# A hybrid encoder layer on one core: a second weight buffer in the first attention block, and attention outputs turned one unit later in another PSUM bank

## The chip, the cores and the metric

The kernel runs on one core of a Trainium2 chip. A core has five engines with queues of their own: TensorE (matrix products; PE in the profile, its weight loads PEld), VectorE (DVE), ScalarE (ACT), GpSimd (POOL) and SyncE (SP, which only issues transfers). They meet at semaphores, and 16 DMA engines move data between HBM and the on-chip memory SBUF. TensorE writes to PSUM, which has eight banks of 512 fp32 columns in each of 128 partitions. The metric is the device time of one execution in microseconds, lower is better.

## What is computed

One step of a layer with 1024 prompt rows and 32 sample rows of 1024 values, all in fp32:

```python
xn = rmsnorm(x, norm1_g);  z = xn @ w_in              # conv B | conv C | conv h | q | k | v | gates
a  = (B * dwconv3_causal(C * h)) @ w_conv_out
q, k = rope(rmsnorm(q)), rope(rmsnorm(k))             # 8 heads, two components of 64 each
o_h = (softmax(Q1 K1^T) - lam * softmax(Q2 K2^T)) V   # chunk-causal; values of 128
b  = (rmsnorm(o, subln_g) * (1 - lam0)) @ w_attn_out
x  = x + (sigmoid(gA) * a + sigmoid(gB) * b) @ w_o
x  = x + PEER(rmsnorm(x, norm2_g))                    # 8 heads choose 16 of 16384 experts each per row
```

PEER takes, for every row and each of its 128 chosen experts, a dot product with one row of a table, a GELU and a gate, and adds as much of a second row. Keys, values and the last two convolution inputs are outputs too.

## The kernel before

**Blocks and stages.** The 1056 rows are nine tiles of 128 (the last has the 32 sample rows), in three blocks of three tiles. Every block goes through an *attention* part and a *middle* part (gates, output projections, second norm, PEER queries and their top 16). The expert work is cut into 1056 *slots*: in slot q POOL gathers for each of 128 rows one 8 KB row pair of the expert table into entry q % 8 of a ring (half of the ring in `mix`, half in `ringx`), VectorE takes the dot product (L1588), ScalarE makes GELU, gate and a diagonal of 64 columns (L1212 to L1223), and TensorE adds the weighed second half to the accumulator in banks 0 and 1 (L1001), or, for a part of the slots, VectorE does (L1599). A ring entry is free for the next gather after that.

**What sets the order.** Each engine's program is one loop over slots from -340 to 1055. The parts of the three blocks are generators that yield a slot number ahead of each step; a step is issued in the loop once its number has passed (`advance`). Steps of one generator keep the order of the code whatever their numbers are. The attention of a block has a table of its own, `ATT` with start and pace: the first block runs in slots -330 to -141, ahead of all gathers, the second in 25.5 to 167, the third in 337 to 513. A *unit* u = 3h + i is head h with tile i of the block; it takes 7 positions, and a position is 1.0, 0.75 or 0.93 of a slot in the three blocks. The constants of lines 48 to 59 give the position of every step in its unit.

**A unit of attention.** TensorE's order in unit u is: scores of u (`score`, L776, both components, into banks 2 to 5), values weighed for u-1 (`weigh_values`, L831, bank 7), queries and keys of u+1 turned (`turn_heads`, L845 and L846, columns 0 to 255 of bank 6), projection of q, k and v for unit u+3 (`project`, L797, columns 0 to 383 of bank 6), in the first block one of three convolution products per tile (`conv_block`, L858), the normalised output of u-1 turned (`turn_out`, L838, bank 4, position `TO`), and the softmax weights of u turned (`turn_weights`, L812, bank 7). ScalarE copies turned heads (`keep_heads`, L1091 and L1092), squares the output (L1065, `square_out`), takes the exponential (L1047), copies and squares new projections (L1081, L1084), copies the turned output (`keep_out`, L1071) and the turned weights (L1060). VectorE takes row maxima (L1395), scales heads (L1446), multiplies the output by its gain (`keep_product`, L1456), forms the difference of the softmaxes (L1404 to L1410), applies the norm (`norm_out`, L1462), and rotates (L1429 to L1435). POOL makes the reciprocal roots (L696 to L707).

Because the turned output goes to bank 4, which the second component's scores use, the turning waits for the exponential of unit u, and the scores of the next unit wait for the copy (`ot_c`). The projection waits for the copies of the turned heads (`tq_c`), since they share bank 6.

**Weights.** `low` holds six blocks of 1024 columns. In the first block its first three hold the q, k and v weights of one head, and the last three those of a convolution channel group; SyncE loads them in the order of `attend(0)`:

```python
                    for h in range(-1, DC):
                        if 0 <= h < DC - 1:
                            for k in range(3):
                                load_conv(h + 1, k)
                        if 0 <= h + 2 < DC:
                            if h >= -1:
                                load_heads(h + 2)
```

`load_conv` waits for the convolution product that used the buffer, `load_heads(g)` for all three projections of head g-1. In the second and third block there are no convolution loads in this part, and even and odd heads have three columns blocks of `low` each.

## Time and profile before

| | us |
|---|---|
| median of 3 runs | 4035.53 |
| the runs | 4030.66, 4035.53, 11249.31 |
| profiled execution | 4040.45 |
| its span (first to last instruction) | 4038.5 |

| engine | busy us | share of the span |
|---|---|---|
| TensorE matmul | 3205.6 | 79% |
| VectorE | 2685.7 | 67% |
| GpSimd | 1550.3 | 38% |
| ScalarE | 1460.6 | 36% |

The core moved 1345 MB; 1107 MB of them are gathers. The mean granted clock of TensorE was 0.866 of full speed. In a row of the timeline the columns are start, duration, engine, line, operation, output and inputs, the number of instructions merged, and in brackets the idle time before it with what ended it. A row of waits says: engine, tile and line that waited, on whom, us in total, number of times, the longest. Busy times are those of one profiled execution.

### The profile page before, as it was taken

How to read it: one execution, taken by the hardware profiler on the slowest of the kernel's cores; microseconds unless marked ns; L12 is line 12 of the kernel's file. 1: busy time of each engine (PE TensorE's matmuls, PEld its weight loads, DVE VectorE, ACT ScalarE, POOL GpSimd, SP SyncE). 2: the span in 40 equal slices, each digit the busy share in tenths (PEclk: the TensorE clock that was granted, in tenths of full speed). 3: DMA queues.
4: the chain of work that ended last, by engine and by line, in shares of the span. 5: the costliest groups of instructions: out<-in, count | busy, mean ns of one | idle time of the engine just before them, and what ended most of it. 6: DMA issues, size and time to landing. Idle time of an engine off the chain costs nothing.

```text
span 4038.5 us, 46682 instructions
## 1 busy us (share of the span) xinstructions
PE 3205.6 (79%) x14264; PEld 1449.4 (36%) x14264; DVE 2685.7 (67%) x6248; ACT 1460.6 (36%) x4353; POOL 1550.3 (38%) x1402
## 2 busy tenths in 40 slices
PE   6888997877886999898788887876779766666666
PEld 3444554433343555344233332544425211111111
DVE  3333103888888976578778886886668864566664
ACT  2111101245665234232456555223433333333332
POOL 1111000344665433333445555443354443444433
...
GB/s 194 78 75 80 126 99 135 294 350 331 356 385 368 410 417 418 380 396 307 313 351 354 387 347 347 416 411 365 406 413 410 366 420 419 420 420 420 410 393 341
DMA packets 258104, 1345.41 MB, mean 333 GB/s; under 512 B 31489, under 2 KB 71169, under 8 KB 122433
## 3 DMA queue, kind: packets, MB, share of 16 engines
...
q1 hardware_dynamic: 80720, 210.05, 14.1%
...
## 4 chain that ended last, share of the span: by engine, by line
PE 40%; DMA 24%; DVE 20%; ACT 5%; issue 4%; DVEq 3%; POOL 2%; SPq 1%; ACTq 1%; POOLq 0%
DMA ringx<-in_peer_uv,tl_idx 12%; DMA mix<-in_peer_uv,tl_idx 10%; PE tl_ps L951 9%; PE tl_ps L1001 7%; PE tl_ps L797 6%; DVE ringx L1588 3%; PE tl_ps L962 3%; PE tl_ps L935 3%; PE tl_ps L986 3%; PE tl_ps L858 3%; DVE mix L1588 3%; DVE tl_xa L1599 2%; PE tl_ps L776 2%; DMA low<-in_watt 1%; DVE tl_mx L1395 1%
## 5 line engine op out<-in xcount | busy, mean ns | idle before, releaser
L734 POOL DMA_INDIRECT mix<-in_peer_uv,tl_idx x528 | 630.7, 1194 | 768.8 <-PE tl_ps L1001 426.2
L734 POOL DMA_INDIRECT ringx<-in_peer_uv,tl_idx x528 | 621.7, 1177 | 722.3 <-PE tl_ps L1001 454.6
L1588 DVE CUSTOM_DVE_ANT_0 mix<-mix,tl_xb 128x1024 f32<-128x1024 f32 x528 | 641.5, 1222 | 281.6 <-DMA mix<-in_peer_uv,tl_idx 273.6
L1588 DVE CUSTOM_DVE_ANT_0 ringx<-ringx,tl_xb 128x1024 f32<-128x1024 f32 x528 | 641.0, 1221 | 271.6 <-DMA ringx<-in_peer_uv,tl_idx 264.0
L1001 PE MATMUL tl_ps<-ringx,tl_dg 64*64 64x512 f32 x3352 | 577.2, 773 | 279.6 <-ACT tl_dg L1223 279.0
L1212 ACT ACTIVATE tl_hg<-tl_hd 128x1 f32<-128x1 f32 x1056 | 213.1, 202 | 1558.4 <-DVE tl_hd L1588 1548.3
L1001 PE MATMUL tl_ps<-mix,tl_dg 64*64 64x512 f32 x3288 | 565.5, 772 | 259.5 <-ACT tl_dg L1223 239.1
L951 PE MATMUL tl_ps<-tl_xr,low 128*128 128x384 f32 (+1 forms) x1280 | 401.0, 469 | 27.2 <-DMA low<-in_wall 22.8
L1216 ACT ACTIVATE tl_hw<-tl_hg,tl_gw 128x1 f32<-128x1 f32 x1056 | 310.9, 294 | 76.2 <-issue 4.7
L1001 PEld LDWEIGHTS tl_ps<-ringx,tl_dg 64*64 64x64 f32 x3352 | 106.3, 156 | 614.8 <-ACT tl_dg L1223 533.4
L797 PE MATMUL tl_ps<-low,tl_xr 128*128 128x384 f32 (+1 forms) x768 | 298.5, 536 | 25.3 <-ACT tl_u L1092 20.1
L951 PEld LDWEIGHTS tl_ps<-tl_xr,low 128*128 128x128 f32 x1280 | 246.6, 196 | 195.8 <-issue 67.7
L1001 PEld LDWEIGHTS tl_ps<-mix,tl_dg 64*64 64x64 f32 x3288 | 105.0, 157 | 588.0 <-ACT tl_dg L1223 482.8
L1223 ACT ACTIVATE tl_dg<-tl_eye,tl_hw 128x64 f32<-128x64 f32 x830 | 288.7, 348 | 59.5 <-issue 2.6
L986 PE MATMUL tl_ps<-tl_xr,low 128*128 128x384 f32 (+1 forms) x768 | 262.1, 480 | 1.9 <-ACTq L1184 1.9
L935 PE MATMUL tl_ps<-tl_xr,low 128*128 128x384 f32 (+1 forms) x768 | 237.1, 467 | 0.6 <-ACT tl_xr L1071 0.6
L797 PEld LDWEIGHTS tl_ps<-low,tl_xr 128*128 128x128 f32 (+1 forms) x768 | 137.0, 189 | 192.8 <-issue 99.7
L705 POOL TENSOR_SCALAR tl_rr<-tl_ss 128x4 f32<-128x4 f32 (+1 forms) x72 | 61.5, 854 | 370.9 <-DVE tl_ss L1416 370.8
L797 PE MATMUL tl_ps<-low,mix 128*128 128x384 f32 x384 | 151.7, 555 | 55.7 <-DMA low<-in_watt 41.6
L986 PEld LDWEIGHTS tl_ps<-tl_xr,low 128*128 128x128 f32 x768 | 139.6, 194 | 135.3 <-issue 75.0
L935 PEld LDWEIGHTS tl_ps<-tl_xr,low 128*128 128x128 f32 x768 | 149.8, 199 | 101.9 <-issue 34.7
L1553 DVE TENSOR_TENSOR tl_u<-tl_ps,tl_u 128x384 f32<-128x384 f32 (+1 forms) x48 | 25.0, 521 | 197.7 <-PE tl_ps L951 195.6
...
## 6 DMA issues: line engine op xcount, KB each, us to landing
...
```

What stands on the lines that cost most here:

```text
L734: nc.gpsimd.indirect_dma_start(out=ring[q % RING].rearrange("p a d -> p (a d)"), out_offset=None, in_=A["peer_uv"], in_offset=bass.Indirec ...
L797: last = nc.tensor.matmul(o, xn[:, c, i * P:i * P + n], w[:, :, c, :], start=(c == 0), stop=(c == DC - 1))
L858: last = nc.tensor.matmul(ps[:, (3, 5, 3)[k], 0:nr], w[:, c, :], xn[:, c, 0:nr], start=(c == 0), stop=(c == DC - 1))
L935: last = nc.tensor.matmul(ps[:, 2 + 3 * (cc % 2) + k, 0:n], w[:, c, :], xnr[:, c, 0:n], start=(c == 0), stop=(c == DC - 1))
L951: last = nc.tensor.matmul(ps[:, 2 + k, 0:n], w[:, c, :], src[k][:, c, 0:n], start=(c == 0), stop=(c == DC - 1))
L962: last = nc.tensor.matmul(ps[:m, 2 + 2 * i + h, :], mixT[:, c, i * P:i * P + m], low_block(keep, (base + 32 + c) % WRING)[:, h * 512:(h + ...
L986: last = nc.tensor.matmul(ps[:, 2 + qb % 2, 0:n], w[:, c, :], xT[:, c, 0:n], start=(c == 0), stop=(c == DC - 1))
L1001: last = nc.tensor.matmul(ps[half_of(h), b, :], dg[rows, npe(q) % DIAGS, :], ring[q % RING][rows, 1, h * 512:(h + 1) * 512], start=k == 0, ...
L1212: nc.scalar.activation(hg[:, j:j + 1], hd[:, j:j + 1], ACT.Gelu)
L1216: gate = nc.scalar.activation(hw[:, j:j + 1], hg[:, j:j + 1], ACT.Copy, scale=gw[:, table(t), k:k + 1])
L1223: nc.scalar.activation(dg[:, npe(q) % DIAGS, :], eye[:], ACT.Copy, scale=hw[:, j:j + 1]).then_inc(s["dg_done"], 1)
L1588: nc.vector.tensor_tensor_reduce(out=ring[q % RING][:, 0, :], in0=ring[q % RING][:, 0, :], in1=xb[:, t % 2, :], scale=1.0, scalar=0.0, op0 ...
```

## The change

Three things are done.

1. In the first block odd heads' weights get a buffer of their own, columns 2304 to 5375 of `ringx` (`heads_at`), behind the rotary tables that lie there. `load_heads(1)` waits for nothing, `load_heads(g)` for the projections of heads up to g-2, and SyncE issues it ahead of the convolution loads of a head. Counts of the semaphores follow.
2. In all blocks the output of unit u-2 is turned in unit u, between the weighing of values and the turning of heads, into columns 384 to 511 of bank 6. ScalarE copies it ahead of the turned heads, once these are in PSUM too. The scores don't wait for that copy any more, the projection does. The last output of a block is turned at its old position.
3. Positions: the turning of heads and the copies of the turned heads move from 1.8 and 2.3 to 0.8 and 1.3, the product of output and gain from 2.2 to 3.2. The scaling of heads stays at 1.0.

```diff
-PV, TO, PJ, TQ, CV = 1.0, 5.0, 2.6, 1.8, 3.6
+PV, TO, PJ, TQ, CV = 1.0, 5.0, 2.6, 0.8, 3.6
-RO, KP = 2.2, 1.2
+RO, KP, SH = 2.2, 2.2, 1.0
...
+        def heads_at(rb, par):
+
+            if rb == 0 and par:
+                return ringx[:, (NT + 1) * 4 * HD:(NT + 1) * 4 * HD + 3 * D]
+            return keep["low"][:, 3 * par * D:3 * (par + 1) * D]
...
             def load_heads(g):
 
-                rb, par = g // DC, g % 2 if g >= DC else 0
-                if rb == 0:
-                    sp.wait_ge(s["pj_done"], 3 * g)
-                elif g % DC == 0:
+                rb, par = g // DC, g % 2
+                if g and g % DC == 0:
                     sp.wait_ge(s["z_done"], BASE[rb])
-                else:
+                elif g > 1:
                     sp.wait_ge(s["pj_done"], 3 * (g - 1))
...
                 if rb == 0:
-                    for h in range(-1, DC):
...
+                    load_heads(1)
+                    for h in range(DC - 1):
+                        if h + 2 < DC:
+                            load_heads(h + 2)
+                        for k in range(3):
+                            load_conv(h + 1, k)
                     return
...
                def score(g, i, components):
-                        if w >= 2:
-                            pe.wait_ge(s["ot_c"], w - 1)
...
                def project(g, i):
                             if j > DC * 3 * rb:
                                 pe.wait_ge(s["tq_c"], max(j - 1, 3 * DC * rb))
+                                if j > 4:
+                                    pe.wait_ge(s["ot_c"], j - 4)
...
-                def turn_out(g, i, seen):
-                    n = rows_of(tiles[i])
+                def turn_out(g, i):
+                    n, latest = rows_of(tiles[i]), min(3 * g + i + 5, 3 * DC * (rb + 1))
                     pe.wait_ge(s["on_d"], 3 * g + i + 1)
-                    pe.wait_ge(s["ex_d"], seen)
-                    nc.tensor.transpose(ps[:, 4, 0:n], on[:n, :], ident[:n, :n]).then_inc(s["to_d"], 1)
+                    for name in ("qn_d", "v_cp", "sq_d"):
+                        pe.wait_ge(s[name], latest)
+                    pe.wait_ge(s["tq_c"], min(3 * g + i + 3, 3 * DC * (rb + 1)))
+                    if 3 * g + i:
+                        pe.wait_ge(s["ot_c"], 3 * g + i)
+                    nc.tensor.transpose(ps[:, 6, 3 * P:3 * P + n], on[:n, :], ident[:n, :n]).then_inc(s["to_d"], 1)
...
+                    if u > 1:
+                        yield step_at(rb, h, base + TQ)
+                        turn_out(DC * rb + (u - 2) // 3, (u - 2) % 3)
                     if -2 < u < 3 * DC - 1:
                         yield step_at(rb, h, base + TQ)
                         turn_heads(DC * rb + (u + 1) // 3, (u + 1) % 3)
...
-                    if u > 0:
+                    if u == 3 * DC:
                         yield step_at(rb, h, base + TO)
...
                 def keep_out(g, i):
                     n = rows_of(tiles[i])
                     act.wait_ge(s["to_d"], 3 * g + i + 1)
-                    nc.scalar.copy(oT[:, g % DC, i * P:i * P + n], ps[:, 4, 0:n]).then_inc(s["ot_c"], 1)
+                    act.wait_ge(s["tq_d"], min(3 * g + i + 4, 3 * DC * (rb + 1)))
+                    nc.scalar.copy(oT[:, g % DC, i * P:i * P + n], ps[:, 6, 3 * P:3 * P + n]).then_inc(s["ot_c"], 1)
...
+                    if u > 1:
+                        yield step_at(rb, h, base + TQ + 0.5)
+                        keep_out(DC * rb + (u - 2) // 3, (u - 2) % 3)
                     if 0 <= after[0] < DC:
                         yield step_at(rb, h, base + TQ + 0.5)
                         keep_heads(DC * rb + after[0], after[1])
```

## Rows read from the trace of the kernel before

**Rows 1.** Stretches: engines' busy us, clock, DMA share, GB/s.
```profile
core 0: us, PE busy (x) PEld busy (x) DVE busy (x) ACT busy (x) POOL busy (x), PEclk, DMA share, GB/s
60.00:425.00 365.00, 308.36 (x1046) 180.69 (x1046) 140.90 (x501) 69.03 (x291) 51.93 (x94) 0.93 0.24 82
812.00:1293.00 481.00, 382.57 (x2024) 175.70 (x2024) 416.59 (x993) 268.09 (x758) 263.65 (x235) 0.90 0.92 356
1880.00:2508.00 628.00, 500.45 (x2545) 201.82 (x2545) 495.01 (x1044) 333.87 (x892) 321.65 (x273) 0.86 0.91 352
3200.00:3900.00 700.00, 439.07 (x2224) 81.78 (x2220) 434.14 (x821) 248.56 (x845) 296.30 (x276) 0.71 1.01 418
```
**Rows 2.** Waits of TensorE, 60 to 425 us: total, times, longest.
```profile
PE tl_ps L797 <- DMA low<-in_watt: 41.6, 7, 6.8
```
**Rows 3.** Timeline of TensorE: projections of one head, and the next.
```profile
264.37 7.97 PE L797 MATMUL tl_ps<-low,mix 128*128 128x384 f32 x16 [6.19 <-DMA low<-in_watt]
...
279.87 5.43 PE L797 MATMUL tl_ps<-low,mix 128*128 128x384 f32 x16 [0.52 <-ACT tl_u L1092]
...
293.27 5.43 PE L797 MATMUL tl_ps<-low,mix 128*128 128x384 f32 x16 [0.52 <-ACT tl_u L1092]
```
**Rows 4.** Timeline of SyncE's queue in that head: the load waited for.
```profile
256.42 1.38 SPq L529 DMA_DIRECT2D low<-in_watt  x3
```
**Rows 5.** Timeline of SyncE's queue at the start of the first block.
```profile
58.01 0.62 SPq L608 DMA_DIRECT2D tl_xr<-xn_t  x1
67.44 1.29 SPq L529 DMA_DIRECT2D low<-in_watt  x3
```
**Rows 6.** Timeline of TensorE: the first projection that waits for weights.
```profile
73.61 6.81 PE L797 MATMUL tl_ps<-low,mix 128*128 128x384 f32 x13 [4.32 <-DMA low<-in_watt]
```
**Rows 7.** Timeline, first block: scores behind idle time (TensorE), copies (ScalarE).
```profile
242.76 0.27 ACT L1071 COPY tl_xr<-tl_ps 128x128 f32<-128x128 f32 x1 [4.72 <-PE tl_ps L838]
...
243.13 0.92 PE L776 MATMUL tl_ps<-tl_u 64*128 64x384 f32 x4 [0.18 <-issue]
...
244.94 0.27 ACT L1091 COPY tl_u<-tl_ps 128x128 f32<-128x128 f32 x1 [1.59 <-PE tl_ps L846]
245.10 0.27 ACT L1092 COPY tl_u<-tl_ps 128x128 f32<-128x128 f32 x1
...
278.01 0.70 PE L776 MATMUL tl_ps<-tl_u 64*128 64x256 f32 x4 [0.29 <-issue]
```
**Rows 8.** Waits of TensorE in the second block, 812 to 1293 us.
```profile
PE tl_ps L838 <- DVE tl_u L1462: 21.6, 9, 5.1
PE tl_ps L797 <- ACT tl_u L1092: 14.1, 10, 4.0
```
**Rows 9.** Waits of VectorE in the second block.
```profile
DVE tl_u L1429 <- ACT tl_u L1084: 11.5, 7, 2.8
DVE tl_u L1456 <- ACT tl_u L1065: 5.7, 2, 3.1
DVE tl_rz L1404 <- ACT tl_u L1047: 5.1, 7, 1.5
```
**Rows 10.** Waits of TensorE in the third block, 1880 to 2508 us.
```profile
PE tl_ps L838 <- DVE tl_u L1462: 16.6, 9, 3.6
PE tl_ps L797 <- ACT tl_u L1092: 6.0, 4, 2.8
```
**Rows 11.** Waits of VectorE in the third block.
```profile
DVE tl_mx L1395 <- PE tl_ps L776: 27.5, 12, 4.7
DVE tl_u L1429 <- ACT tl_u L1084: 23.9, 13, 6.2
DVE tl_u L1456 <- ACT tl_u L1065: 16.0, 10, 4.7
DVE tl_rz L1404 <- ACT tl_u L1047: 13.0, 9, 2.2
DVE ringx L1588 <- DMA ringx<-in_peer_uv,tl_idx: 6.6, 4, 2.5
```
**Rows 12.** A wait of ScalarE in the second block.
```profile
ACT tl_u L1091 <- PE tl_ps L846: 12.8, 13, 2.5
```

21 lines of the change are left out of this document (7 added, 14 removed).

## The prediction

> **What bounds the kernel now.** I read the stage table first (busy time per engine, granted clock, DMA share by stretch), because what a saved microsecond is worth depends on the stage. It shows three regimes [rows 1]. From 60 to 425 us the first block's attention runs alone: TensorE is busy 308 of 365 us, DMA is nearly idle at 0.24, and no expert rows are gathered yet, so the stretch is a chain on TensorE. From 812 to 1293 us and from 1880 to 2508 us the attention of the second and the third block runs between the gathers: DMA share 0.92 and 0.91 at 356 and 352 GB/s, VectorE 417 of 481 and 495 of 628 us. From 3200 to 3900 us the DMA is full (1.01, 418 GB/s); nothing on an engine is worth anything there. The bounds of the mixed stretches are the slots of the step tables (25.5 to 167 and 337 to 513), counted off by VectorE's dot products. So the change, which touches attention only, can pay in the first stretch fully and in the two mixed ones as far as DMA and VectorE allow. Everything behind runs by slot number and not by the clock, so a saved microsecond moves all that follows; the next weights' loads move with it.
>
> The waits of TensorE in the first stretch come next: 41.6 us in seven waits for head weights [rows 2]. The timeline shows what one costs [rows 3]: the projection at 264.37 starts after 6.19 us of idle, and its 16 matmuls then take 7.97 us, where the unstalled ones (279.87, 293.27) take 5.43 and wait only 0.52 us for a ScalarE copy. Start to start, unstalled units are 13.40 us apart (279.87 to 293.27). Why the weights are late: SyncE works its queue in order, its last convolution load waits until the block's third convolution product is done, and the three head loads stand behind it, issued at 256.42, when they need about 8 us to land [rows 4]. With one buffer they could not go before the projection that reads it had ended in any case.
>
> Last I read who makes TensorE and VectorE wait in the mixed stretches. TensorE waits 21.6 and 16.6 us at the turning of the outputs (L838) for their normalisation on VectorE, and 14.1 and 6.0 us before a projection for the copies of the turned heads [rows 8, 10]. VectorE hardly waits for gathers there (6.6 us of 628 for the ring's second half in the third block); its waits are those inside attention [rows 9, 11].
>
> **Part 1: second buffer in the first block.** Odd heads' weights go to columns 2304 to 5375 of the ring, which gathers fill only after the first block. The first odd load waits for nothing now; its neighbours in SyncE's queue are the table stores and one reload issued at 58 us, and today it is issued at 67.44 and waited for from 69.29 (73.61 - 4.32) [rows 5, 6]. A load takes about 8 us from issue to use [rows 4], so it arrives in time or within 1 us of it. Later loads wait for the projections of two heads before, and come ahead of the convolution loads in the queue, so they have one whole head period (some 40 us) to land. The convolution loads now stand behind a wait for projections that end before the convolution product they wait for, and they are wanted 35 us later: cost nothing, covered by the period. The same bytes move, at a DMA share of 0.24. Removed: 41.6 us of waits less 7 x 0.52 us, the copy wait that then ends last, is 38.0 us. The slow matmuls too: in the row at 264.37 they cost 7.97 - 5.43 = 2.54 us. The granted clock of the stretch is 0.93 [rows 1]: TensorE falls from its level of 2.4 GHz to that of 1.2 GHz in the six microseconds without matmuls, and the first part of the next projection is run there; behind the waits of 0.52 us no projection is slow. With the stalls gone I take all of it: 7 x 2.54 = 17.8 us. Part 1: 55.8 us. Bounds: 38.0 (the clock falls anyway) to 56.
>
> **Part 2: outputs turned one unit later, in bank 6.** *In the first block.* The scores start 0.18 to 0.29 us after the weight transposes, because today the copy of the turned output out of bank 4 must be done [rows 7]; that wait goes, 23 times 0.23 us, 5.4 us. The transposition itself only moves, from ahead of the scores to behind them, on the same chain. Added is one more ScalarE copy ahead of the two that the next projection waits for anyway; such copies start 0.16 us apart (244.94, 245.10) [rows 7]: 23 x 0.16 = 3.7 us. Net gain 1.7 us; bounds -4 (nothing of the first is seen) to +5. The wait for the normalised output is away by construction: it is a unit (13 us) old.
>
> The rule that speaks against this part is that of the Trainium skill, page "PSUM — Partial Sum Buffer", section "PSUM bank collisions raise a hardware error": two engines may not be in one bank and quadrant at once, even on different columns, so the free columns of bank 6 are not a free bank. Read strictly, no copy may overlap another engine's work in the bank and each is paid whole: by the rows 0.27 in place of 0.16 us, 6.2 in place of 3.7 us, and part 2 would lose 1 us here in place of winning 1.7. The copies in the rows overlap with each other, being of one engine, so I stay with 0.16.
>
> *In the second and third block.* TensorE loses its waits of 21.6 + 16.6 us at L838, and the 14.1 + 6.0 us before projections shrink, since the turning of heads moves from position 1.8 to 0.8 of the 7 positions of a unit (a position is 0.75 and 0.93 of a slot there) while the projection stays at 2.6. But TensorE is not what ends last; it is busy 383 of 481 us and then waits for ScalarE's slot weights. So I count what VectorE, the busiest at 0.87, stops waiting for. L1456 (output times gain) moves from 2.2 to 3.2, and ScalarE's square that it waits for moves from 2.3 (behind the copies of the heads) to 1.6: all of 5.7 and 16.0 us go [rows 9, 11]. L1404 waits for the exponential, which stood behind the same copies and the square, about 0.5 us of copies: I take 4 of 5.1 and 8 of 13.0. L1429 waits for the projection: with 36 us of TensorE's waits gone in the second block I take 8 of 11.5, in the third, where only 23 go, 12 of 23.9. Row maxima waiting for scores in the third block: most of the 27.5 I put down to the sample tile's second component, which waits for the first one's exponential; 7. Sum 18 + 43 = 61 us. Half of it I give back: a VectorE that comes earlier meets the next wait earlier, and DMA has only 8 to 9% to give. That leaves 30 us. Bounds: none of it (0) to 61 us, and as a ceiling the DMA rate of the full stretches, 481 x (1 - 356/418) + 628 x (1 - 352/418) = 71 + 99 us.
>
> Queues: SyncE's loads in these blocks stay in place. ScalarE gets the output copy ahead of the head copies, one of 0.27 us and in the place of one that it had later; behind it stand square, exponential and the slot's gate. POOL's order is unchanged; its reciprocal root of the output now finds the square done earlier.
>
> **Sum.** 55.8 + 1.7 + 30 = 87.5 us. The profiled execution took 4040.45 us (span 4038.5), 4.9 us over the median of 4035.53; 4040.5 - 87.5 = 3953 on its scale, 3948 on that of the median.
>
> **Rivals.** (All on the median's scale.)
> *A, only part 1 pays: 4035.5 - 57.5 = 3978 us, chance 0.31.* For it: DMA share 0.92 is close to full, and TensorE is not the bound in the mixed stretches, so its waits may only change names. Against: VectorE, not the gathers, is waited for there. [...]
> *B, the mixed stretches give all of it: 4035.5 - 57.5 - 61 = 3917 us, chance 0.17.* For it: the ceiling of 170 us leaves room, and the clock of these stretches (0.90, 0.86) may rise with fewer gaps. Against: four waits in a row rarely all go.
> *C, slower: 4098 us, chance 0.05.* One mechanism: ScalarE. The copies and the square move up by a position, to 0.2 to 0.6 of a slot behind TensorE's weighing, which so far lay about one slot ahead. If ScalarE then stands behind TensorE in each unit for weighing and transposes (its wait at L1091 is 12.8 us in 13 cases now [rows 12]), gates and slot weights come late. At 2.5 us in each of 48 units that is 120 us less 57.5. It decides from 57.5/48 = 1.2 us a unit.
> *D, the stalls stay (another wait in SyncE's queue holds the loads): 4035.5 - 31.7 = 4004 us, chance 0.05.* Nothing in the queue's rows speaks for it but the order itself.
> The forecast has 0.42, with a range of its own of 3925 to 3968.
>
> **How the numbers follow.** 2% (about what a measurement of this kernel can tell from no change) is 80.7 us, so "faster" begins below 3955. The forecast lies on that line: about 0.6 of its 0.42 is below, with B's 0.17 and a little of A that is 0.45. Slower by over 2% would need 4116, beyond C's price: 0.03. The rest, 0.52, is within 2%. The range runs from 3905 (past B's 3917) to 3990 (past A's 3978); C, D and the tails outside it are no more than 2 in 10.
>
> **What the profile after would show.** Part 1 is right if the waits of L797 for head weights are gone, all projections of the first block after the fourth take 5.4 us, the clock from 60 to 425 us is near 1.0, and all of the first block's attention ends some 57 us earlier. Part 2 is right if L838 shows no wait for L1462, L1456 none for L1065, and the second and third block's stretches are shorter by 30 us together at a higher DMA share. A is right if these waits are gone and the stretches as long as before. C shows as ScalarE waiting at L1091 or L1065 for over a microsecond in each unit. The forecast is wrong in its main term if matmuls stay slow with no stall ahead of them, or if the first odd load lands late; and in its second if VectorE's waits return under other names.

## The result and the profile after

| | before | after |
|---|---|---|
| median, us | 4038.84 (all its runs beside the other) | 3988.48 (3981.49 to 3999.82) |
| ratio, 95% interval | | 0.9885 [0.9847, 0.9923] |
| profiled execution, us | 4040.45 | 3982.71 |
| its span, us | 4038.5 | 3980.8 |

The change gives 50 us by the medians and 57.7 by the two profiled executions, where 87.5 were forecast. Two more sets of runs of the same kernel (below) give 3986 and 3991. In the text, lines of the kernel after stand with their numbers there: the projection is L799 (was L797), the turning of outputs L844 (L838), turned heads L851 and L852 (L845, L846), the slot's weighing L1010 (L1001), the copies L1081, L1101 and L1102 (L1071, L1091, L1092), the square L1074 (L1065), the exponential L1056 (L1047), the rotation L1442 (L1429), the output's product L1469 (L1456), the difference L1417 to L1423 (L1404 to L1410), the norm L1475 (L1462), row maxima L1408 (L1395), the dot product L1601 (L1588).

**Where the time went, stage by stage.** Everything behind the first block runs by slots, so I time each kernel by the start of VectorE's dot product of a slot in its timeline. One profiled execution each, in us:

| stretch | before | after | gain | forecast |
|---|---|---|---|---|
| start to slot 0 (first block's attention and middle) | 704.8 | 653.9 | 50.9 | 57.5 |
| slots 25 to 167 (second block's attention) | 481.3 | 478.4 | 2.9 | } 30 |
| slots 337 to 513 (third block's attention) | 611.8 | 609.6 | 2.2 | } |
| the other slots, up to the last | 2227.7 | 2226.1 | 1.6 | 0 |

The same stretches in the stage table of the kernel after answer to [rows 1]:

```profile
core 0: us, PE busy (x) PEld busy (x) DVE busy (x) ACT busy (x) POOL busy (x), PEclk, DMA share, GB/s
60.00:374.00 314.00, 291.39 (x1046) 171.99 (x1046) 142.17 (x500) 67.63 (x289) 51.89 (x94) 0.99 0.28 96
763.80:1242.10 478.30, 376.79 (x2026) 172.86 (x2026) 417.26 (x983) 266.32 (x761) 257.94 (x235) 0.91 0.92 359
1832.10:2441.70 609.60, 477.86 (x2496) 196.31 (x2496) 482.00 (x1012) 328.22 (x883) 313.14 (x271) 0.89 0.90 351
3200.00:3900.00 700.00, 442.93 (x2192) 82.34 (x2192) 422.78 (x794) 245.62 (x831) 292.05 (x272) 0.69 1.00 411
```

The same 1046 matmuls of the first block fit into 314 us instead of 365, at a granted clock of 0.99 instead of 0.93. In the two mixed stretches hardly a number moves.

**The first block.** TensorE's waits there (total, times, longest) answer to [rows 2], its timeline to [rows 3] and [rows 6]:

```profile
PE tl_ps L799 <- ACT tl_u L1102: 15.5, 21, 0.8
PE tl_ps L799 <- DMA ringx<-in_watt: 3.0, 1, 3.0
```
```profile
60.00 5.43 PE L799 MATMUL tl_ps<-low,mix 128*128 128x384 f32 x16 [0.52 <-ACT tl_u L1102]
...
70.35 7.78 PE L799 MATMUL tl_ps<-ringx,mix 128*128 128x384 f32 x16 [2.98 <-DMA ringx<-in_watt]
...
112.17 5.40 PE L799 MATMUL tl_ps<-low,mix 128*128 128x384 f32 x16 [0.79 <-ACT tl_u L1102]
...
374.69 7.09 PE L960 MATMUL tl_ps<-mix,low 128*128 128x384 f32 x16 [0.66 <-ACT tl_xr L1081]
```

Six of the seven stalls are gone, and with them the slow projections. One is left, the first: 2.98 us of wait and a projection of 7.78 us. The last row is the first matmul of the middle part; before, its like started at 425.76, so the attention ends 51.1 us earlier.

How a stall makes a projection slow can be read from the granted clock of the kernel before, around the projection of [rows 3] at 264.37 (columns as in [rows 1]; the granted clock is the third figure from the right):

```profile
250.00:258.00 8.00, 7.92 (x35) 4.97 (x33) 4.48 (x15) 1.30 (x4) 1.74 (x2) 1.00 0.11 27
260.00:264.00 4.00, 0.00 (x0) 0.00 (x0) 0.96 (x4) 0.00 (x0) 0.00 (x0) 0.84 0.68 274
264.00:269.00 5.00, 4.63 (x7) 2.52 (x8) 0.00 (x0) 0.00 (x0) 0.00 (x0) 0.50 0.00 0
270.00:275.00 5.00, 5.00 (x17) 2.96 (x16) 1.57 (x5) 0.55 (x2) 0.23 (x1) 1.00 0.00 0
```

TensorE is busy at 1.00 (the level of 2.4 GHz), stands idle, the clock falls within the idle time, the first 5 us of the projection run at 0.50 (1.2 GHz), and then it is back at 1.00. But a stall is not the only thing behind which a projection is slow. The prediction says that behind waits of 0.52 us none is; the trace of the kernel before has one, in the same place as the first row above:

```profile
60.23 7.12 PE L797 MATMUL tl_ps<-low,mix 128*128 128x384 f32 x16 [0.52 <-ACT tl_u L1092]
```

It took 7.12 us, that of the kernel after 5.43. Further executions of the kernel after (e0, e16) have 7.12 there again, so this is scatter between executions and not part of the gain. SyncE's queue shows why the first stall stays (answers to [rows 5]):

```profile
57.40 0.62 SPq L611 DMA_DIRECT2D tl_xr<-xn_t  x1
60.52 1.46 SPq L533 DMA_DIRECT2D ringx<-in_watt  x3
65.46 1.28 SPq L533 DMA_DIRECT2D low<-in_watt  x3
```
```profile
SPq L533 <- DMA rope_rows<-ringx: 2.5, 1, 2.5
60.52:70.35 9.83, 5.74 (x22) 3.07 (x20) 4.15 (x18) 1.90 (x8) 2.01 (x3) 0.90 1.02 388
```

The load waits for nothing of its own, but SyncE's queue ahead of it waits for the stores of the normalised rows and of the rotary tables to land (the first row of these two is a wait of SyncE's queue), so it goes out at 60.52, a mere 7 us earlier than at 67.44. From there to its use it takes 9.8 us, where 8 were taken from [rows 4]: in this window (second row) the DMA share is 1.02, not the 0.24 that is the mean of the whole stretch.

**The mixed stretches.** TensorE's waits, then VectorE's, in the second block (763.8 to 1242.1 us; answers to [rows 8, 9]):

```profile
PE tl_ps L1010 <- ACT tl_dg L1236: 66.9, 38, 7.3
PE tl_ps L814 <- DVE tl_u L1423: 11.9, 7, 3.1
PE tl_ps L799 <- ACT tl_u L1102: 5.5, 4, 3.0
...
DVE tl_u L1442 <- ACT tl_u L1094: 11.9, 7, 3.9
DVE tl_rz L1417 <- ACT tl_u L1056: 8.2, 6, 2.4
```

and in the third (1832.1 to 2441.7 us; answers to [rows 10, 11]), with ScalarE's largest in attention:

```profile
PE tl_ps L1010 <- ACT tl_dg L1236: 79.1, 48, 6.9
...
DVE tl_mx L1408 <- PE tl_ps L777: 23.9, 9, 6.1
DVE tl_u L1442 <- ACT tl_u L1094: 23.8, 13, 4.9
DVE tl_rz L1417 <- ACT tl_u L1056: 21.0, 10, 3.3
DVE ringx L1601 <- DMA ringx<-in_peer_uv,tl_idx: 9.2, 7, 2.6
DVE tl_u L1469 <- ACT tl_u L1074: 6.4, 2, 3.6
...
ACT tl_xr L1081 <- PE tl_ps L852: 65.5, 20, 9.4
```

The waits that the change aimed at are gone or small: L844 waits for no norm in the mixed stretches (21.6 and 16.6 us before; of the 16.6 in the window of [rows 10], 13.0 fall in slots 337 to 513), L799 for copies 5.5 us and none (14.1, 6.0), L1469 for squares 0 and 6.4 (5.7, 16.0). In their place TensorE waits longer for ScalarE's slot weights (66.9 and 79.1 us, was 46.3 and 65.2) and newly for the difference (L814, 11.9 us), and VectorE waits for the exponential 8.2 and 21.0 us, was 5.1 and 13.0.

The account that makes these stretches readable is VectorE's own. Its busy time, all its waits for others, and a rest (issue, and gaps too short to be listed) make up the stretch:

| kernel, stretch | length | VectorE busy | its waits | rest |
|---|---|---|---|---|
| before, second | 481.3 | 417.2 | 29.3 | 34.8 |
| after, second | 478.4 | 417.3 | 26.2 | 34.9 |
| before, third | 611.8 | 482.0 | 98.5 | 31.3 |
| after, third | 609.6 | 482.0 | 96.2 | 31.4 |

Work and rest are fixed to 0.1 us here, so the stretch changes by what the *total* of VectorE's waits changes. The sum itself is an identity and says nothing of causes; what it shows is that no wait of the list can be booked as a gain unless the total falls with it. The forecast had taken 43 us out of the third block's 98.5 in its list, and halved the sum; the total fell by 2.3.

### The profile page after: what moved, and what is told of

Its sections match the earlier page's. It is cut to its first block, busy times and chain, and to the rows that moved or that the text cites. A ratio compares the mean times of both kernels' runs of the same rounds, so it can differ in the third digit from the quotient of the medians.

```text
span 3980.8 us, 46892 instructions
## 1 busy us (share of the span) xinstructions
PE 3171.0 (80%) x14264; PEld 1436.5 (36%) x14264; DVE 2687.4 (68%) x6248; ACT 1454.3 (37%) x4353; POOL 1531.0 (38%) x1402
## 4 chain that ended last, share of the span: by engine, by line
PE 40%; DMA 25%; DVE 19%; ACT 6%; issue 4%; DVEq 3%; POOL 1%; ACTq 1%; SPq 0%; POOLq 0%
DMA mix<-in_peer_uv,tl_idx 11%; DMA ringx<-in_peer_uv,tl_idx 11%; PE tl_ps L960 9%; PE tl_ps L1010 8%; PE tl_ps L799 5%; PE tl_ps L995 4%; PE tl_ps L971 3%; PE tl_ps L864 3%; DVE ringx L1601 3%; DVE mix L1601 3%; DVE tl_xa L1612 2%; PE tl_ps L944 2%; PE tl_ps L777 2%; PE tl_ps L833 1%; ACT tl_u L1056 1%
## 5 line engine op out<-in xcount | busy, mean ns | idle before, releaser
L737 POOL DMA_INDIRECT mix<-in_peer_uv,tl_idx x528 | 621.0, 1176 | 783.5 <-PE tl_ps L1010 430.4
L1601 DVE CUSTOM_DVE_ANT_0 mix<-mix,tl_xb 128x1024 f32<-128x1024 f32 x528 | 640.6, 1222 | 286.9 <-DMA mix<-in_peer_uv,tl_idx 278.7
L1601 DVE CUSTOM_DVE_ANT_0 ringx<-ringx,tl_xb 128x1024 f32<-128x1024 f32 x528 | 640.9, 1222 | 279.0 <-DMA ringx<-in_peer_uv,tl_idx 271.8
L1010 PE MATMUL tl_ps<-ringx,tl_dg 64*64 64x512 f32 x3352 | 579.3, 777 | 300.4 <-ACT tl_dg L1236 300.2
L1010 PE MATMUL tl_ps<-mix,tl_dg 64*64 64x512 f32 x3288 | 561.2, 768 | 276.9 <-ACT tl_dg L1236 253.4
L960 PE MATMUL tl_ps<-tl_xr,low 128*128 128x384 f32 (+1 forms) x1280 | 402.6, 471 | 25.2 <-DMA low<-in_wall 22.7
L1010 PEld LDWEIGHTS tl_ps<-ringx,tl_dg 64*64 64x64 f32 x3352 | 107.6, 156 | 642.9 <-ACT tl_dg L1236 568.0
L1010 PEld LDWEIGHTS tl_ps<-mix,tl_dg 64*64 64x64 f32 x3288 | 104.9, 156 | 614.4 <-ACT tl_dg L1236 504.9
L799 PE MATMUL tl_ps<-low,tl_xr 128*128 128x384 f32 (+1 forms) x768 | 292.9, 528 | 10.0 <-ACT tl_u L1102 5.5
L799 PEld LDWEIGHTS tl_ps<-low,tl_xr 128*128 128x128 f32 (+1 forms) x768 | 135.3, 186 | 183.6 <-issue 98.3
L1612 DVE SCALAR_TENSOR_TENSOR tl_xa<-mix,tl_hw,tl_xa 128x1024 f32<-128x1024 f32 x117 | 149.9, 1281 | 3.7 <-issue 3.4
```

Of the source, the lines that this page charges most:

```text
L737: nc.gpsimd.indirect_dma_start(out=ring[q % RING].rearrange("p a d -> p (a d)"), out_offset=None, in_=A["peer_uv"], in_offset=bass.Indirec ...
L799: last = nc.tensor.matmul(o, xn[:, c, i * P:i * P + n], w[:, :, c, :], start=(c == 0), stop=(c == DC - 1))
L960: last = nc.tensor.matmul(ps[:, 2 + k, 0:n], w[:, c, :], src[k][:, c, 0:n], start=(c == 0), stop=(c == DC - 1))
L1010: last = nc.tensor.matmul(ps[half_of(h), b, :], dg[rows, npe(q) % DIAGS, :], ring[q % RING][rows, 1, h * 512:(h + 1) * 512], start=k == 0, ...
L1601: nc.vector.tensor_tensor_reduce(out=ring[q % RING][:, 0, :], in0=ring[q % RING][:, 0, :], in1=xb[:, t % 2, :], scale=1.0, scalar=0.0, op0 ...
L1612: nc.vector.scalar_tensor_tensor(out=xa[:], in0=ring[q % RING][:, 1, :], scalar=hw[:, k % TOPK:k % TOPK + 1], in1=xa[:], op0=ALU.mult, op1 ...
```

## The experiments

Two theories stood at the start (the expectations, quoted below as they were on record, work them out). **T1:** the first block pays 51 us, the mixed stretches next to nothing, as the gathers (DMA share 0.92) set their length (rival A). **T2:** the mixed stretches are a chain through VectorE, ScalarE and TensorE, in which removed waits come back elsewhere; then some edit of the chain must move them where halved transfers do not. The table gives all kernels; the columns of stretches are as above, of one profiled execution each. Each ratio is to runs of the kernel before on the same chip. The medians come from four groups of runs: e0 to e3; e5 and e7 to e9; e6, e10, e11 and, on the same chip, e16 to e18; e12 to e15. The kernel before had 4037.5, 4040.5, 4038.3 and 4040.3, and 4039.6 in them; "gain" below is the distance to that. A single stretch scatters between executions of one kernel: the changed kernel has 478.4, 477.8, 477.6 and 609.6, 608.4, 620.0 in three, and the second block took 476.6, 474.7 and 481.5 in e6, e17 and e12, which differ in no more than one load of the first block. So 5 us in the second block and less than 10 in the third say nothing alone. e7 and e9 leave work out and return wrong values; they are measurements only.

| kernel | median | ratio [95%] | slot 0 | second | third |
|---|---|---|---|---|---|
| before | 4037.5 to 4040.5 | 1 | 704.8 | 481.3 | 611.8 |
| e0_after | 3986.3 | 0.9879 [0.9856, 0.9901] | 653.0 | 477.8 | 608.4 |
| e16_after_again | 3990.9 | 0.9874 [0.9859, 0.9889] | 654.2 | 477.6 | 620.0 |
| e1_buffer_only | 3992.8 | 0.9895 [0.9870, 0.9919] | 654.6 | 481.4 | 614.2 |
| e2_turn_only | 4035.3 | 0.9993 [0.9981, 1.0005] | 703.1 | 480.7 | 611.6 |
| e3_after_first_early | 3982.8 | 0.9862 [0.9838, 0.9886] | 649.7 | 477.8 | 616.8 |
| e7_half_gathers | 3985.8 | 0.9864 [0.9842, 0.9885] | 654.0 | 480.8 | 608.6 |
| e8_no_vector_adds | 3974.6 | 0.9836 [0.9814, 0.9858] | 654.1 | 471.4 | 611.4 |
| e9_no_table_switch | 3962.1 | 0.9805 [0.9785, 0.9824] | 655.7 | 470.1 | 590.5 |
| e5_after_old_positions | 3999.0 | 0.9894 [0.9877, 0.9910] | 654.7 | 486.9 | 615.4 |
| e6_buffer_new_positions | 3980.5 | 0.9856 [0.9837, 0.9875] | 654.7 | 476.6 | 605.0 |
| e17_positions_again | 3983.2 | 0.9866 [0.9850, 0.9881] | 654.7 | 474.7 | 602.5 |
| e15_buffer_product_later | 3988.1 | 0.9872 [0.9857, 0.9887] | 656.4 | 483.5 | 604.0 |
| e14_positions_only | 4029.1 | 0.9975 [0.9966, 0.9984] | 701.2 | 476.7 | 604.3 |
| e10_exp_first | 4081.7 | 1.0108 [1.0086, 1.0129] | 692.0 | 530.3 | 619.0 |
| e13_copy_behind_square | 4017.3 | 0.9947 [0.9933, 0.9960] | 672.0 | 484.5 | 611.8 |
| e11_best | 3978.2 | 0.9844 [0.9824, 0.9864] | 651.4 | 474.8 | 616.0 |
| e12_positions_first_early | 3979.0 | 0.9858 [0.9843, 0.9873] | 650.4 | 481.5 | 603.6 |
| e18_all_gains | 3967.0 | 0.9826 [0.9813, 0.9840] | 652.2 | 469.7 | 602.6 |

### The two parts alone

The changed kernel as it is, the kernel before with the second buffer alone (part 1), and the changed kernel without it (parts 2 and 3: the `load_heads` and `attend(0)` of before).

> The changed kernel once more, so that the parts below stand beside it on the same chip. Theory 1 (all of the gain is the weight buffer in the first block; the turning only renames waits): ratio to before 0.986 to 0.989, the first gather's dot product about 51 us earlier than before (slot 0 at 654 us), and the distance from slot 25 to 513 within 8 us of before's 1684 us. Theory 2 (the turning gives 30 us and the first result had bad luck): ratio 0.980 or below.

> Only the second buffer for head weights and the order of the loads in the first block; outputs turned as before, positions as before. Theory 1: within 0.2% of the changed kernel (ratio to before 0.986 to 0.989), and in the first block 2 to 4 us better than it, since each projection waits 0.52 us for the copies and not 0.75 to 0.80: last projection to last projection in the steady part 39.6 us a head, not 39.9. Theory 2: half of the changed kernel's gain or less, 20 us slower than it.

> Only the later turning in bank 6 with the new positions, one weight buffer in the first block as before. Theory 1: 0 to -8 us against before, ratio 0.998 to 1.001; the seven stalls stay (41 us), TensorE has no wait at the turning, and VectorE's wait for the output square is mostly gone while its wait for the exponential grows from 5 and 13 us to 8 and 20 us in the two mixed stretches. Theory 2: -30 us, ratio 0.992.

The buffer alone gives 45 us by the medians and 50.2 in the first block (704.8 to 654.6), its mixed stretches as long as before. The later turning with its positions gives 2 us or nothing (0.9993, interval on both sides of 1).

In the first block, slot 0 does not separate the two turnings: with the buffer it lies at 653.0 to 655.7 us in seven executions with the later turning and at 654.6 to 656.4 in four with the old one. e1 was expected 2 to 4 us earlier than the change and is not. The attention itself does separate them. Over 19 units, from the projection that starts at 85.3 us in the kernel after to the last one at 338.1, it takes 251.3 us in all six executions with the old turning and the buffer, and 252.9 to 253.1 in nine with the later turning. So the later turning *costs* 1.7 us there. Slot 0 hides it: the end of the attention is 0.4 us shorter with the later turning, and the middle part behind it, which no edit touches, took 278.6 to 279.2 us with it and 280.4 to 280.6 in five of the six others (e12: 279.2); why is not known.

### The first stall

The first odd load is issued ahead of the table stores:

```diff
+            for k in range(3):
+                sp.dma_start(heads_at(0, 1)[:, k * D:(k + 1) * D], A["watt"][3 + k]).then_inc(s["a_in1"], 16)
             sp.dma_start(A["xn_t"], parts(keep["mix"], 0, DC, ROWS)).then_inc(s["xn_out"], 16)
...
-                    load_heads(1)
```

> The changed kernel with the first odd head's weights issued at the very start of SyncE's second program, ahead of the store of the normalised rows (before 43 us and not at 60 us). The first projection from the new buffer waited 2.98 us in the changed kernel and ran 7.78 us in place of 5.43. If the late load is the cause of both: the wait falls to the 0.5 us of the copies, the projection to 5.4 us, and slot 0 comes 4.8 us earlier (ratio to the changed kernel 0.9988). Rival: the projection stays slow (7.1 to 7.8 us), since TensorE is little busy at the start of the block whatever the load does: 2.5 us only.

TensorE's timeline of that kernel (where the projection is L800) shows the first projection from the new buffer:

```profile
68.98 5.40 PE L800 MATMUL tl_ps<-ringx,mix 128*128 128x384 f32 x16 [0.57 <-issue]
```

The wait is gone, and the projection takes 5.40 us in place of 7.78. Slot 0 comes 3.3 to 4.5 us earlier, where 4.8 were expected. That the late load caused the slow matmuls too is not shown, though. Three more kernels have the early load (e11, e12, e18, below). In e12 the projection takes 5.40 us as here; in e11 and e18 it takes 7.09 behind a wait of 0.57 us, which is what the rival in the expectation said. This is e11:

```profile
68.45 7.09 PE L800 MATMUL tl_ps<-ringx,mix 128*128 128x384 f32 x16 [0.57 <-issue]
```

The place of the weights is not the cause (both happen with weights in `ringx`). In both e3 and e11 TensorE is idle for 1.12 us and then for 0.57 just before it, and only in e11 does the clock fall. So the early load is worth the wait (1.3 to 2.4 us in three executions of the change), and whether it also saves slow matmuls differs from execution to execution; e11, with the later turning like e3, has slot 0 at 651.4, 1.6 to 2.8 us earlier than the change.

### Are the mixed stretches bound by the gathers, by VectorE, or by ScalarE?

Three kernels take work away from one engine each, on top of the change. The first halves each gathered row pair, the second gives VectorE's additions in the slots of the two attention parts to TensorE, the third keeps ScalarE on one function table:

```diff
-                    out=ring[q % RING].rearrange("p a d -> p (a d)"), ... in_=A["peer_uv"],
+                    out=ring[q % RING][:, 0, :] if mixed else ..., in_=A["peer_uv"].rearrange("e (a d) -> (e a) d", a=2) if mixed else ...,
```
```diff
-SHARED = ((0,170,1,6),(170,300,3,4),(336,520,1,6),(520,680,2,3))
+SHARED = ((0,24,1,6),(170,300,3,4),(520,680,2,3))
```
```diff
-... ACT.Exp, scale=QKS,
+... ACT.Exp if rb == 0 else ACT.Gelu, scale=QKS,
```

> The changed kernel with gathers of 4 KB per row in place of 8 KB in slots 25 to 167 and 337 to 513; it leaves out the second half of each row there (the dot products see other rows, the adds stale ones), nothing else. Rival A (the gathers bound the two stretches, at a DMA share of 0.90 to 0.92): they shrink from 478 and 609 us by 50 us or more each, down to VectorE's 417 and 482 us busy. Theory of the engines' chain (in-order engines waiting for each other, the gathers covered): both stretches stay within 15 us, at a DMA share near 0.5.

> The changed kernel with no expert rows added by VectorE in slots 24 to 169 and 336 to 519: TensorE does all of them. VectorE loses about 24 adds of 1.28 us in the second block's stretch (31 us) and 29 in the third's (37 us); TensorE gets as many matmul groups of 1.1 us and ScalarE as many diagonals of 0.35 us. If VectorE's busy time sets the stretches: 25 to 35 us shorter each. If it is the chain through all of them: 0 to 15 us shorter. If TensorE sets them: 10 to 25 us longer.

> The changed kernel with the attention's exponential in the second and third block replaced by a GELU of the same operands, which is in the function table that the slots use: it leaves out the two table loads of 1.28 us per unit (61 us of ScalarE in each stretch) and gives other values. If ScalarE's lateness is what VectorE's waits for the exponential (8 and 21 us) and for the squares of the projections (12 and 24 us) come from: both stretches shrink by 20 to 50 us. If VectorE's own work sets them: by the 8 and 21 us at most. If the gathers do: not at all.

The stage table of the kernel with half gathers, second and third block:

```profile
763.00:1242.00 479.00, 381.42 (x2024) 175.85 (x2024) 415.38 (x985) 263.89 (x754) 255.81 (x234) 0.90 0.62 204
1833.00:2442.00 609.00, 478.20 (x2491) 195.41 (x2491) 481.81 (x1010) 326.06 (x880) 310.17 (x270) 0.88 0.61 205
```

DMA falls from a share of 0.92 to 0.62 and from 359 to 204 GB/s, and the stretches keep their length. T1's reason is out: the bytes of the gathers do not set it (their number is the same). VectorE's waits for gathers in the third block all but went, from 13.2 us to 0.6, and its total stayed (96.2 and 95.8): those for row maxima and the exponential rose from 23.9 and 21.0 to 30.4 and 24.1. This is the plainest case of a wait that comes back under another name.

Without VectorE's additions, VectorE's largest waits in the second block:

```profile
DVE tl_u L1442 <- ACT tl_u L1094: 22.4, 10, 4.4
DVE tl_rz L1417 <- ACT tl_u L1056: 14.8, 11, 2.8
```

They were 11.9 and 8.2. VectorE's work falls from 417 to 392 us, its waits in all rise from 26 to 45 us, the stretch is 7 us shorter. In the third block 31 us of work go and 33 of waits come: nothing. VectorE is busy for 0.87 of the second stretch, and most of the work taken from it turns into waits for others.

The stage table with one function table on ScalarE:

```profile
765.00:1236.00 471.00, 379.26 (x2039) 175.65 (x2042) 417.81 (x987) 207.33 (x715) 259.75 (x236) 0.91 0.93 363
1828.00:2419.00 591.00, 471.49 (x2508) 198.17 (x2512) 482.08 (x1012) 243.95 (x822) 319.42 (x271) 0.89 0.94 364
```

ScalarE's work falls by 59 and 84 us, the stretches by 8 and 19: the only one of the three that shortens both, though ScalarE, at 0.56 and 0.54, is the least busy of TensorE, VectorE and itself. VectorE's waits fall to 18.6 and 77.6 us. It is the wait for the exponential that goes, from 8.2 and 21.0 to 2.0 and 4.2 us, while that for the projections' squares stays (11.9 and 27.1, was 11.9 and 23.8). So here a removed wait *was* paid out: 6.2 and 16.8 us went, and the stretches are 8.3 and 19.1 us shorter. The expectation's first case, 20 to 50 us from each stretch, missed; its second, at most the 8 and 21 us of the exponential, has the numbers. T2 holds as far as this: the latency through ScalarE's queue is part of the chain, and a full DMA or a busy VectorE is not the whole of it. The table loads can't be left out in a right kernel, so this is a measurement and no gain.

### Which half of the edit of turning pays?

The change moves two things in the mixed stretches: *positions* (heads turned at 0.8 instead of 1.8, product of output and gain later) and the *turning* (unit u-2 instead of u-1, bank 6 instead of 4). These kernels are the other corners; every one but the last has the second buffer.

```diff
 e5_after_old_positions: the changed kernel with the old positions
-PV, TO, PJ, TQ, CV = 1.0, 5.0, 2.6, 0.8, 3.6
+PV, TO, PJ, TQ, CV = 1.0, 5.0, 2.6, 1.8, 3.6
-RO, KP, SH = 2.2, 2.2, 1.0
+RO, KP, SH = 2.2, 1.2, 1.0
 e6_buffer_new_positions, e17_positions_again: before, with buffer; e14_positions_only: without
-PV, TO, PJ, TQ, CV = 1.0, 5.0, 2.6, 1.8, 3.6
+PV, TO, PJ, TQ, CV = 1.0, 5.0, 2.6, 0.8, 3.6
-RO, KP = 2.2, 1.2
+RO, KP = 2.2, 2.2
-                        yield step_at(rb, h, base + TQ - 0.8)
+                        yield step_at(rb, h, base + 1.0)
 e15_buffer_product_later: before, with buffer, of these only
-RO, KP = 2.2, 1.2
+RO, KP = 2.2, 2.2
```

> The changed kernel with the old positions (turning of heads 1.8, copies 2.3, product of output and gain 2.2), so that only the place and time of the output's turning differ from a kernel with the buffer alone. Measured so far, slots 25 to 167 take 481 us before and 478 us after, slots 337 to 513 take 612 and 609 us. If the order alone brings the 3 us of the second block: 478 us and 609 us stay. If the new positions do: 481 us, and VectorE's wait for the output square is back (6 and 16 us). Either way the whole is within 0.2% of the changed kernel.

> The fourth corner: second buffer, outputs turned as before in bank 4, but the new positions (turning of heads 0.8, copies 1.3, product of output and gain 3.2). The corners so far, slots 25 to 167 and 337 to 513: old order and old positions 481 and 614 us, new order and old positions 487 and 615, new order and new positions 478 and 608 to 610. If the positions pay by themselves: about 475 and 608 us and a whole at least as fast as the changed kernel (3986 us on its last chip). If the new order is what makes room for them: 481 us or more and 612 or more, 5 to 10 us slower than the changed kernel, with TensorE's wait for the normalised output as large as before or larger, since its input is made later (21 and 13 us).

> The kernel before with the new positions alone (turning of heads 0.8, copies 1.3, product 3.2), one buffer, old turning. From the corners: slots 25 to 167 in 477 us, 337 to 513 in 605 to 608, the first block as before: 8 to 12 us faster than before, ratio 0.9975. If it is scatter: ratio 0.999 to 1.001.

> Second buffer, old turning, and of the new positions only the later product of output and gain (3.2); the turning of heads and its copies stay at 1.8 and 2.3. If the gain of the positions is VectorE's wait for the square (6 and 16 us) that goes: stretches 477 and 607 us, 3982 us in all. If it is the earlier turning of heads, with more work between it and the projection: 481 and 613, 3991 us in all, with VectorE's waits moved from the product to the exponential.

> The changed kernel, beside the next two on one chip. 3985 to 3989 us as in its two results so far.

> Second buffer, new positions, outputs turned as before. If the later turning costs what the corners say (two pairs of medians: 3999.0 against 3992.8 at the old positions, 3986.3 against 3980.5 at the new): 5 to 7 us faster than the changed kernel beside it. If it costs nothing: within 3 us of it.

| with the buffer: median, second + third stretch | old positions | new positions |
|---|---|---|
| turning in bank 4, unit u-1 | 3992.8, 481 + 614 | 3980.5 and 3983.2, 477 + 605 and 475 + 603 |
| turning in bank 6, unit u-2 | 3999.0, 487 + 615 | 3986.3 and 3990.9, 478 + 608 and 478 + 620 |

The positions give 8 to 13 us in both rows, and without the buffer 10: positions alone 0.9975 [0.9966, 0.9984], an interval clear of 1. The cost of the later turning is smaller than what one pair can show: the ratios' intervals overlap in every pair, and with the old positions the two ratios are all but equal (0.9894 and 0.9895). But all pairs that differ in it alone lean the same way. In gain over the kernel before on the same chip, the old turning is ahead by 3 us at the old positions (e1, e5), 6 to 9 at the new (e6 and e17 against the change), 8 without the buffer (e14, e2), 6 with the early load (e12, e3) and 13 with that and fewer additions (e18, e11). For the pair measured side by side the medians are 3990.9 and 3983.2, though single runs overlap (3983.8 to 3993.2 and 3973.6 to 3989.7).

The third block shows it best. With the new positions, five executions with the old turning (e6, e17, e12, e14, e18) took 602.5 to 605.0 us in slots 337 to 513, and seven with the later one (the change and e0, e16, e2, e3, e11, e7) 608.4 to 620.0. In the second block nothing separates them (474.7 to 481.5 and 477.6 to 480.8; e11 and e18, with fewer additions, 474.8 and 469.7). Two expectations missed on the way: e5 was to lie within 0.2% of the changed kernel and has a second stretch of 487 us, longer than both its cases; e12 was to be 10 us faster than the change with 477 us in the second stretch, and is 4 us faster than e3 by the medians, within its rival's 5, with 481.5.

In the kernel with buffer and new positions (e6; turning is L840, the norm L1464, the exponential L1049, the difference L1406) these are waits of TensorE and VectorE in the second block:

```profile
PE tl_ps L840 <- DVE tl_u L1464: 21.8, 10, 5.8
...
DVE tl_rz L1406 <- ACT tl_u L1049: 4.4, 5, 1.5
```

TensorE's wait of 21.8 us for the norm is there as before, and the stretch is no longer than with the change, which removes it: removing it in this way bought nothing. VectorE's wait for the rotation is 11.7 us here and 11.9 with the change, so it did not hang on TensorE's wait at the turning. VectorE's wait for squares is gone from the list (5.7 us before), so the positions alone removed it. In the third block the same kernel has

```profile
DVE tl_rz L1406 <- ACT tl_u L1049: 18.3, 10, 3.3
...
DVE tl_u L1458 <- ACT tl_u L1067: 3.2, 1, 3.2
```

where the change has 21.0 and 6.4. This difference is in every execution: exponential and squares together are 20.6 to 22.7 us in the five with the old turning, and 26.6 to 29.0 in the change, e0, e16, e2, e3 and e11. The other corner, old positions with the new turning (e5), shows where the turning presses in the second block:

```profile
PE tl_ps L799 <- ACT tl_u L1102: 26.3, 16, 4.9
...
DVE tl_u L1469 <- ACT tl_u L1074: 7.8, 3, 4.6
```

The projection waits for copies 26.3 us, was 14.1. Moving only the product later (e15) gives 4.7 us by the medians against the buffer alone, with intervals that overlap: part of what the positions give. In the third block it has all of it (604.1, as with all new positions, against 614.2; squares 5.7 us, was 16.7), in the second none (483.5).

### ScalarE's order of work

If the exponential comes late because copies and the square stand ahead of it, it should help to put it first, or to put the output's copy behind the square:

```diff
 e10_exp_first: exp_scores moved ahead of keep_out and keep_heads
+                    if here:
+                        yield step_at(rb, h, base + TQ + 0.5)
+                        exp_scores(g, i, (0,) if t == NT else (0, 1))
                     if u > 1:
                         yield step_at(rb, h, base + TQ + 0.5)
                         keep_out(DC * rb + (u - 2) // 3, (u - 2) % 3)
 e13_copy_behind_square: keep_out moved behind square_out, nothing else
```

> The changed kernel with ScalarE's exponential of a unit ahead of the copies of the turned output and heads and of the square, in all blocks. Theory: VectorE's wait for the exponential (8 and 21 us in slots 25 to 167 and 337 to 513) stands for TensorE's turning of heads, behind which ScalarE waits (24 and 68 us at the first copy). Then the exponential comes earlier, this wait falls under 4 and 8 us, but the copies come 1.4 to 3 us later and each projection with them (the two table loads of 1.28 us now lie ahead of the copies): TensorE's wait before projections grows from 6 us to 30 us or more a stretch, and VectorE's for the projections' squares with it. Stretches 478 and 609: between 10 us shorter and 10 us longer; the first block 1 us or more per unit slower (20 to 30 us in all), since there the chain on TensorE is uncovered. Rival (the wait is for ScalarE's own work alone): stretches 8 and 20 us shorter.

> The changed kernel with ScalarE's copy of the turned output moved from ahead of the copies of the heads to behind them and the square. If the later turning costs its microseconds through this copy, which lies ahead of head copies, square and exponential: VectorE's waits for the exponential and the square fall to those of the kernel with the old turning and new positions (4 and 18 us, and none), the stretches go from 478 and 609 to 477 and 605. If through TensorE (a transposition ahead of the turning of heads, and a projection that waits for one more copy): no change, 478 and 609; in the first block each projection then waits 0.2 us longer (1.0 us), since the square now lies in between: 4 us lost there.

With the exponential first, TensorE's largest wait in the second block is

```profile
PE tl_ps L799 <- ACT tl_u L1102: 71.4, 21, 8.8
```

where it was 5.5, and the stretch is 52 us longer; in the first block 38 us are lost. The direction was expected, the size in the second block missed. ScalarE's waits there show a cause that the expectation did not have:

```profile
ACT L1056 <- DVE tl_nb L1410: 41.6, 22, 6.4
```

The exponential needs VectorE's row maxima (L1410). At its new place it stands 41.6 us for them, 1.1 with the change, and the copies stand behind it. The projections need the copies far more urgently than VectorE needs the exponential.

Behind the square, the copy costs 29 us against the change, where at most 4 were expected. ScalarE's own timeline in the first block shows what had been overlooked (ACTq is its queue issuing a transfer):

```profile
211.37 0.38 ACTq L1111 DMA_DIRECT2D out_k_prompt<-tl_u  x1
211.78 0.51 ACTq L1111 DMA_DIRECT2D out_v_prompt<-tl_u  x1
212.33 0.53 ACTq L1117 DMA_DIRECT2D kt_rows<-tl_u  x1
212.90 0.28 ACT L1074 ACTIVATE tl_u<-tl_ps 128x128 f32<-128x128 f32 x1 [1.16 <-issue]
213.17 0.26 ACT L1081 COPY tl_xr<-tl_ps 128x128 f32<-128x128 f32 x1
```

Between the copies of the heads and the square lie, in every third unit, three stores of keys and values, issued from ScalarE's queue at 0.4 to 0.5 us each. The copy now stands behind them, and the projection that waits for it starts after 2.26 us of idle in this unit, in place of 0.75 to 0.79. Of 22 projections six have such a wait (2.25 to 2.55 us), and three of these six then take 7.09 us; most others wait 0.99 to 1.25, about the 0.2 us more that were expected. Together this is about the 18 us by which slot 0 is later. In the mixed stretches the move brought nothing back: VectorE's wait for squares in the third block is 5.9 us (6.4 with the change), though the copy no longer stands ahead of the square. For the exponential this run says nothing, since the copy still stands ahead of it.

### Putting gains together

The first adds to the changed kernel the early load and takes VectorE's additions out of the second block's slots. The second has buffer, new positions and the old turning, with the early load. The third has all four: buffer, new positions, early load, no additions on VectorE in slots 24 to 169, and the old turning in bank 4.

```diff
+SHARED = ((0,24,1,6),(170,300,3,4),(336,520,1,6),(520,680,2,3))
```

> The changed kernel with two edits that gained by themselves: the first odd head's weights issued at the start, and no expert rows added by VectorE in slots 24 to 169 (in the third block they stay). If the gains add: slot 0 at 649.7 us (4 us earlier than the changed kernel), slots 25 to 167 in 471 us in place of 478, the rest as it was: 11 us under the changed kernel, ratio to before 0.985. Rival (one of both was the scatter of one profile): ratio 0.987 or above.

> Second buffer, new positions, the first odd head's weights issued at the start; outputs turned as before in bank 4. If the later turning costs what the four corners say (6 to 10 us over both stretches) and the early load gives its 4 us: slots 25 to 167 in 477 us, 337 to 513 in 605, slot 0 at 650.5, and 3975 to 3978 us in all, ratio to before 0.9845, 10 us faster than the changed kernel. Rival (the corners' differences are scatter): within 5 us of the changed kernel with the early load (3983 us).

> Second buffer, new positions, old turning, first odd head's weights issued at the start, no expert rows added by VectorE in slots 24 to 169. If the gains of the parts add up (early load 4 us, no adds 3 to 7 us on top of the kernel beside it): 3970 to 3974 us. If they share a limit: 3976 to 3980.

The first comes out as forecast (0.9844 for 0.985), the second 1 to 4 us slower than forecast. The third is the fastest that computes everything: 3967.0 us, 0.9826 [0.9813, 0.9840], 24 us under the changed kernel beside it (e16) and 73 under the kernel before, a little better than the 3970 to 3974 expected. It does without the change's second part.

## Why the prediction was right and wrong

**Part 1, 55.8 forecast, 50.2 measured (buffer alone, start to slot 0).** The mechanism is right: six waits for weights gone, the projections behind them at 5.40 to 5.43 us, clock at 0.99, no wait of TensorE for convolution loads. These six alone, added up from the trace before, are 37.3 us of waits less 6 x 0.52, and 47.7 us of projections less 6 x 5.43: 49.3 us. The mis-sized term is the first stall. I took a load issued "in time or within 1 us of it" and counted seven stalls; it goes out at 60.6 behind SyncE's waits for the stores and takes 9.9 us to its use on a full DMA. The kernel with the buffer alone has

```profile
70.47 8.32 PE L799 MATMUL tl_ps<-ringx,mix 128*128 128x384 f32 x16 [2.46 <-DMA ringx<-in_watt]
```

That is 2.46 - 0.52 = 1.9 us of wait and 8.32 - 5.43 = 2.9 us of slow matmuls, 4.8 of the 5.6 us that are missing. The stall got shorter, from 4.32 us [rows 6], and its projection no faster (7.78 before). How much of the 2.9 us is owed to the late load is open, since in two of four kernels with the early load the projection is still slow. The sentence "behind the waits of 0.52 us no projection is slow" is wrong: the two of [rows 3] are not, the one at 60.23 is.

**Part 2 in the first block, a gain of 1.7 forecast, a loss of 1.7 measured over 19 units of its attention.** Slot 0 does not show it, for the reason given above. The wait of the scores is gone, but the projection's went from 0.52 and 0.57 to 0.75 and 0.79: by 0.22 to 0.23 us, where the forecast had priced the copy at 0.16. That alone takes all of the 0.23 us a unit that the forecast credited to the scores. The copies do start 0.16 us apart in the kernel after (124.52, 124.68, 124.84 in ScalarE's timeline). What makes up the 0.09 us a unit lost beyond that is open; the transposition, put at nothing because it only moves, is a candidate. The strict reading of the Trainium skill's page "PSUM — Partial Sum Buffer", section "PSUM bank collisions raise a hardware error", would have made it a loss of 1 us, nearer to what the runs show; but all three copies are one engine's and do overlap, so this agreement is luck and nothing here tests that rule.

**Part 2 in the second and third block, 30 forecast, 5.1 measured in the two stretches of this execution (-5 and 7 in two more), 5 to 7 by the medians' gains over the buffer alone.** This is the step that failed, in two places. First, *I added up VectorE's waits as if each were time to be had.* Of the 61 us, the squares' 5.7 + 16.0 went in part (to 0 and 6.4), the wait at the rotation stayed (11.5 to 11.9, 23.9 to 23.8), the row maxima, from which I took 7, scatter about their 27.5 (23.9, 24.5 and 30.8 in three executions), and the wait for the exponential, from which I took 4 and 8, rose by 3 and 8. The total over all of VectorE's waits fell by 3.1 and 2.3 us, and that is what the stretches gained. "Half of it I give back" was a guess with no row under it; nine tenths came back. Second, *I counted TensorE's waits at the turning as a cause of VectorE's.* They went, but TensorE's waits in sum did not fall: in the second stretch 94 us before and 101 after, as the slot weights took their place. And the kernel with new positions and the old turning keeps this wait at 21.8 us, has the same wait at the rotation and is no slower. What pays are the positions (8 to 13 us), of which the prediction spoke only as a detail, and the later turning, the main thing in it, costs some 3 to 13, in most pairs 6 to 8.

**Where the later turning costs is shown, by what means is not.** Most of it is in the third block, where VectorE waits some 6 us more for ScalarE's exponential and squares; 1.7 us are in the first. Two things could make ScalarE late: its copy ahead of the copies of the heads, or TensorE's transposition and its waits ahead of the turning of heads. In the old positions TensorE's wait at the projection doubles (14.1 to 26.3); with the new ones it is 5.5 us and the cost is still there. e13 moved the copy behind the square and the squares came no earlier (5.9 for 6.4 us), which speaks against the copy for that wait; TensorE's order was not tried by itself. It stays open.

**The rivals.** A's number, 3978, is nearest the 3988 measured. One of its reasons is right, that TensorE's waits would only change their names; the other, DMA near its limit, is wrong: halving the gathers moves nothing. The page "Perfetto Trace Analysis" of the Trainium skill, section "Identifying the Most-Contended Engine", says to work first on the engine of the highest occupancy; among VectorE, ScalarE and GpSimd that is VectorE (0.87 of the second stretch). In this case's runs, less work on it (392 for 417 us) gives 7 us of the second stretch and nothing of the third, while less work on ScalarE, busy 0.56 and 0.54, gives 8 and 19. B needed all waits to go; none of the total did. C's sign appeared without its loss: in the third block ScalarE stands 65.5 us at L1081 behind TensorE, 2.7 us for each of 24 units (41 us in all at its first copies before), and the slot weights' longer wait (79.1 for 65.2 us) took the place of others instead of lengthening the stretch. D is out.

**The range** of 3905 to 3990 holds the median, at its very edge. That it holds it is luck: it was set by the rivals' numbers, and its centre rested on a sum of waits.
